# Layer 0's attention jobs: one whole job per projection unit in place of half a job

## The reference, cut to what matters

```python
proj = x @ w_in + b_in
q, k, v, h, gb, gc = jnp.split(proj, [o1, o2, o3, o4, o5], axis=-1)
...
part = banded_window_attn(q, k, v, 1, A_WINDOW, slopes)     # prompt: keys t-128..t, ALiBi
part = gathered_window_attn(q, k_all, v_all, n_hist, 1, A_WINDOW, slopes)   # samples, with a cache
y_a = combine_branches([part], sink=sink)     # softmax with a learned sink in the denominator
c = gc * h
conv = sum(c_all[:, i:i + T] * conv_w[i] for i in range(CONV_WIDTH))
y_b = gb * conv
mix = jnp.concatenate([y_a, y_b], axis=-1) @ w_out + b_out
```

## Time and profile before

| what | value |
|---|---|
| time, median of 3 runs | 2876.88 us (2871.78 to 2877.8) |
| span of the profiled execution | 2878.8 us; no other time of that execution is given |
| TensorE busy | 2724.0 us, 95% of the span |
| VectorE, ScalarE, GpSimd busy | 1022.6, 601.8, 520.3 us |
| mean granted TensorE clock | 0.973 |
| units 24 to 53 of layer 0 | from 119.81 us on |
| first store after them | 354.40 us |

### The profile page before, as it was taken

One profiled execution on the slowest core, in us unless ns is written; L12 is line 12 of the kernel. 1 busy time (PEld: TensorE's weight loads), 2 busy tenths in 40 slices (PEclk: granted clock), 3 DMA queues, 4 the chain that ended last, 5 costly groups with the idle time before them and its releaser, 6 DMA issues.

```text
span 2878.8 us, 40841 instructions
## 1 busy us (share of the span) xinstructions
PE 2724.0 (95%) x16564; PEld 2544.3 (88%) x16564; DVE 1022.6 (36%) x2244; ACT 601.8 (21%) x1297; POOL 520.3 (18%) x319
## 2 busy tenths in 40 slices
PE   7999778999999999989998999989899999999997
PEld 7989678899999999988995666669799999999996
DVE  3344325322222222264245455542722222222225
ACT  1022201411221112212002232330322111221121
POOL 2111012312121212133111000001322121212120
PEclk9999789999999999999998999999999999999998
DMA  5100031212232223212107243421113222322221
GB/s 166 58 30 30 18 80 47 84 64 92 78 116 68 90 75 116 73 66 92 37 30 225 96 147 96 140 86 58 54 64 117 68 92 73 116 73 89 78 95 63
DMA packets 79066, 240.19 MB, mean 83 GB/s; under 512 B 25568, under 2 KB 43616, under 8 KB 71648
## 3 DMA queue, kind: packets, MB, share of 16 engines
q1 hardware_dynamic: 61376, 167.65, 17.4%
q10 hardware_dynamic: 17584, 71.05, 8.3%
HBM read 224.78 MB, written 81.71 MB: 106 GB/s over the span
## 4 chain that ended last, share of the span: by engine, by line
PE 82%; DVE 8%; issue 4%; ACT 3%; DMA 2%; POOL 1%; SPq 0%; POOLq 0%; DVEq 0%; ACTq 0%
PE PS L1151 65%; PE PS L1531 2%; PE PS L1498 2%; PE PS L1467 2%; PE PS L1439 2%; PE PS L1482 1%; PE PS L1452 1%; DVE ZN L762 1%; PE PS L1180 1%; POOL WS L418 1%; DVE X L741 1%; ACT SMA L555 1%; PE PS L1238 1%; PE PS L1281 1%; DVE SMA L834 1%
## 5 line engine op out<-in xcount | busy, mean ns | idle before, releaser
L1151 PE MATMUL PS<-XS,WS 128*128 128x384 f32 (+1 forms) x8208 | 1395.8, 330 | 68.8 <-DVE XS L720 25.3
L1151 PEld LDWEIGHTS PS<-XS,WS 128*128 128x128 f32 x8208 | 1370.3, 190 | 76.9 <-issue 73.6
L1151 PE MATMUL PS<-HID,WS 128*128 128x384 f32 (+1 forms) x4608 | 765.1, 326 | 4.0 <-DVE X L941 4.0
L1151 PEld LDWEIGHTS PS<-HID,WS 128*128 128x128 f32 x4608 | 758.3, 188 | 6.1 <-DVE X L941 5.7
L418 POOL TENSOR_TENSOR WS<-WR,WS 128x1024 fp32r<-128x1024 f32 x178 | 431.0, 2421 | 1812.2 <-DVE WS L732 1060.2
L941 DVE TENSOR_TENSOR X<-X,PS 128x384 f32<-128x384 f32 (+1 forms) x384 | 203.2, 532 | 461.1 <-PE PS L1151 461.1
L926 DVE TENSOR_TENSOR HID<-ST,HID 128x384 fp32r<-128x384 f32 (+1 forms) x192 | 104.3, 543 | 632.7 <-ACT HID L604 632.7
L598 ACT ACTIVATE RT<-PS 128x384 f32<-128x384 f32 (+1 forms) x192 | 90.9, 474 | 1113.4 <-PE PS L1151 1113.4
L674 ACT ACTIVATE PTD<-PS 128x512 f32<-128x512 f32 (+2 forms) x96 | 46.9, 489 | 253.0 <-PE PS L1452 253.0
L602 ACT ACTIVATE ST<-RT 128x384 f32<-128x384 f32 (+1 forms) x192 | 97.5, 508 | 7.8
L604 ACT ACTIVATE HID<-ST 128x384 fp32r<-128x384 f32 (+1 forms) x192 | 97.5, 508 | 6.1
(11 more groups left out here) (170 smaller groups left out, 1625.4 us busy)
## 6 DMA issues: line engine op xcount, KB each, us to landing
WR<-in_w SPq DMA_DIRECT2D x178, 512.0 KB, 3.3
out_d_ks<-in_cache_d_k ACTq DMA_DIRECT2D x96, 340.0 KB
out_d_vs<-in_cache_d_v ACTq DMA_DIRECT2D x96, 340.0 KB
KCD<-in_cache_d_k SPq DMA_DIRECT2D x16, 1024.0 KB, 4.9
VCD<-in_cache_d_v SPq DMA_DIRECT2D x16, 1024.0 KB, 6.7
X<-in_x SPq DMA_DIRECT2D x4, 1536.0 KB, 9.9
TH<-in_th SPq DMA_DIRECT2D x8, 512.0 KB, 5.1
KCD<-in_cache_d_k SPq DMA_DIRECT2D x32, 128.0 KB, 4.1
```

Of the source, the lines that this page charges most:

```text
L1151: last = pe.matmul(out[:, 0:gw], WS[:, slot, a, (off + k) * P:(off + k + 1) * P], src[:, b, k, c0:c0 + gw], start=(n == 0), stop=(n == 3 * ...
```

## The change

TensorE now takes, after unit 24 + v, the odd slot 2v - 1 and the even slot 2v together: transposes of job v-1 (and transposed outputs where due), values of job v-1, and scores of job v. So job v's scores stand behind unit 24 + v for v from 0 to 16, the sample job's values behind unit 41, its transposed outputs behind unit 42. Units 43 to 53 have no attention work, and none stands behind unit 53. VectorE does the same: after every unit's evacuation from unit 24 on, `a_output` of the job before and `a_scores` of the job, and a last `a_output` after unit 41. ScalarE's, GpSimd's and SP's programs are not altered.

```diff
@@ VectorE
-                        if s >= 2:
-                            v = u - 24
-                            if v % 2 == 0:
-                                if v:
-                                    a_output(v // 2 - 1)
-                                a_scores(v // 2)
+                        if 0 <= u - 24 < N_JOBS_A:
+                            if u > 24:
+                                a_output(u - 25)
+                            a_scores(u - 24)
+                        if u - 24 == N_JOBS_A:
+                            a_output(N_JOBS_A - 1)
             for g in range(3):
                 for j in range(2):
                     u = 48 + 2 * g + j
                     ein_evac(16 + j, g, u)
                     if g == 2:
                         w_high(16 + j + NSLOT)
-                    v = u - 24
-                    if v % 2 == 0:
-                        a_output(v // 2 - 1)
-                        a_scores(v // 2)
-            for n in range(15, N_JOBS_A):
-                a_output(n - 1)
-                a_scores(n)
-            a_output(N_JOBS_A - 1)
             split_low(1, Y)
@@ TensorE
             for s in range(2, 4):
                 for g in range(3):
                     for j in range(4):
-                        unit(12 * s + 4 * g + j, 4 * s + j, g)
-                        a_slot(12 * (s - 2) + 4 * g + j)
+                        v = 12 * (s - 2) + 4 * g + j
+                        unit(24 + v, 4 * s + j, g)
+                        if 0 < v <= N_JOBS_A:
+                            a_slot(2 * v - 1)
+                        if v < N_JOBS_A:
+                            a_slot(2 * v)
+                        elif v == N_JOBS_A:
+                            a_values(N_JOBS_A - 1)
+                        elif v == N_JOBS_A + 1:
+                            pe.wait_ge(oa_evac, N_JOBS_A)
+                            pe.wait_ge(ota_evac, 8)
+                            for quad in range(2):
+                                last = pe.transpose(PS[:, 5, quad * P:quad * P + P], OTA[:, quad, :], IDN[:, :])
+                            last.then_inc(ota_mm, 1)
             for g in range(3):
                 for j in range(2):
                     unit(48 + 2 * g + j, 16 + j, g)
-                    a_slot(24 + 2 * g + j)
-            for n in range(15, N_JOBS_A):
-                a_slot(2 * n)
-                a_slot(2 * n + 1)
-            a_values(N_JOBS_A - 1)
-            pe.wait_ge(oa_evac, N_JOBS_A)
-            pe.wait_ge(ota_evac, 8)
-            for quad in range(2):
-                last = pe.transpose(PS[:, 5, quad * P:quad * P + P], OTA[:, quad, :], IDN[:, :])
-            last.then_inc(ota_mm, 1)
```

## The result

The kernel with whole jobs took 2902.32 us (median; 2895.53 to 2908.01), the kernel before beside it 2875.84: a ratio of 1.0088, with a 95% interval of 1.0067 to 1.0109. It is slower, by more than the range of the prediction allowed. A second measurement gave 2898.53 against 2878.22 (1.0074, 1.0060 to 1.0088). The profiled execution took 2895.53, its span is 2893.7, 14.9 more than before. (In every run shown here the time of an execution is 1.7 to 1.9 us over its span.)

The account below looks back on a forecast made before the run. TensorE mostly bounds the kernel, and SP's first store sets the end; some 36 of the tail's 42 us are spent again among the units, the rest at SP. Stores leave 0.3 earlier: 2876.9 - 0.3, or 2877 us; range 2871 to 2888.

Parts of the forecast that it names:

- The loop: TensorE's repeat per job among the units: 6.40 scores to transposes, 2.21 to values, 1.93 to next scores, 10.54 us.
- job 2's scores: Start of the fourteen loops on TensorE, put at 139.5 us: 146.55 - 8.3 + 1.3.
- the forecast without a fall: Granted clock stays full among the units; 2877 us, the likeliest case, chance 0.35.
- two falls or more: Rival: granted clock drops to 1.2 GHz among the units at least twice; two give 2885, four 2893; chance 0.25.
- the tail's idle 1.66 and second wait at 314 to 318: Argument against clock drops: behind the last unit, before the change, values after these waits still ran at full pace, 2.00 us.
- The rival's price: Cost of one clock drop among the units, through slower unit, values and scores: 1.1 to 5.5 us, taken as 4.
- the four slots with 320 columns: Slots among the units called worst for clock drops, having 0.69 us idle besides the copy wait.
- The sample's values: Sample job's 64 matmul records on TensorE: 6.0 us, between 5.65 and 7.0; by themselves should not lower the clock.
- SP's queue: Before the first store, tile 23 waits for GpSimd's split of tile 21: 9.2 us after unit 52 hands over at 344.9.
- The cast of tile 21: Weight cast near the units' end, claimed hidden under GpSimd's work on tile 20; otherwise costing up to 0.7 us.
- VectorE's split of Y: Split for the out projection, claimed to start a few us before the stores and hide under the reload.
- the predicted 354.1: Time in us at which SP's first store leaves, 344.9 + 9.2, against 354.40 before.

Follow-up runs that it names:

- with the stores first: Changed kernel with SP's loads of weight tiles 22 and 23 moved behind the issue of the stores: 2894.24 us, 1.0051 of the kernel before.
- the two of one kernel: Two profiled executions of the changed kernel altered to half a job per unit in the first 23 units, whole jobs in the next six: medians 2880.26 and 2873.32 us.
- the kernel with spare products: Changed kernel plus six unused 256-column matmuls behind each job's transposes, during TensorE's wait for ScalarE's copy: 2885.22 us, 1.002 of the kernel before.

## Why the prediction was wrong, point by point

- **The loop** was right: 10.54 predicted and measured, with 6.40, 2.21 and 1.93 in it, and the waits of 1.11 and 0.68. From job 2's scores (140.09, predicted 139.5) to the sample's (298.52) it is 158.43: fourteen loops of 10.53 are 147.4, and the four falls the other 11.0.
- **The failed step** is in the rivals and the chances: that the forecast without a fall has 0.35, and two falls or more 0.25. The argument against falls was that the tail's idle 1.66 and second wait at 314 to 318 were still followed by values at full pace. That was one passage, and it says nothing of sixteen on end, which the change makes. (The slow values behind it in the earlier trace rows, 3.67, do not settle it either: TensorE was idle for 4.40 before the transposes at 324.62, and in that idle time, between 321 and 322, the clock fell.) What the runs show in its place: four or five falls ahead of the sample's values in each of the three profiled executions that have whole slots only and nothing in the waits (the changed kernel twice, and with the stores first), each costing 1.3 to 2.9, and one more about the sample's values. Whether a given slot has a fall varies from execution to execution, as the two of one kernel show. The rule of the Trainium skill that stood beside this rival ("TensorE: Matmul & The Clock Gate", "A second HAM failure mode: psum-queue depth-cycling"), a clock that swings where TensorE idles briefly again and again, agrees with what these runs show: 0.7 to 1.1 us of idle in a slot of 10.5, and a clock that goes to 0.50 and back.
- **The rival's price**, 4 us a fall, was too high in the loop: 1.6 with a half-wide job, 2.2 and 2.9 else. Its mechanism, slower scores and a slower unit, was right; the values stayed at 2.00. That the four slots with 320 columns would be the worst was wrong: in the first execution one of the four has a fall, and three of the ten others.
- **The sample's values** were predicted at 6.0, at most 7.0, and measured at 9.36. At full pace 64 records of 0.114 are 7.3, so the row of 110 ns was the right end to take, not half of the slow time; the fall inside adds 2.1, and 2.0 to the unit behind. That these values by themselves should not lower the clock was wrong: in the kernel with spare products no wait stood ahead of them, and it fell. The unbroken work of the earlier trace rows had 128 columns to a load, these have 64; broken into quarters they kept the clock. That the number of columns decides was not tried alone.
- **SP's queue** was right as a mechanism: GpSimd's split of tile 21 is the last wait, and moving the two loads gains some 5 to 6 with whole jobs and nothing in the kernel before. Its size was off: 11.35 from unit 52's hand-over (360.88 to 372.23) for 9.2. The cast of tile 21, said to be hidden under the split of tile 20, started 0.30 into it and took 2.60 in place of 0.69; GpSimd waited 0.63 for it, inside the 0.7 that the prediction allowed. The split of tile 21 took 3.80 in place of 2.35 beside VectorE's split of Y, which the prediction had put at nothing.

The sum of it: the store came 18.1 after the predicted 354.1. Falls are 16.6 of that (1.6, 2.2, three times 2.9, and 4.1 about the sample's values); 2.15 are the splits and 1.3 the sample's full pace; off go 1.0 for an earlier start of unit 24 (118.81, before 119.81) and 0.7 for the sample's softmax (7.87 from scores to values for 8.6). These terms come to 0.2 more than the 18.1. The reload's way to TensorE is 1.2 longer, the rest of the kernel 4.1 shorter: 15.2 over the forecast, 14.9 over the span before. The medians lie further apart, 26.5. The profiled execution of after is 6.8 under its median, its fellows having a mean clock of 0.968 to 0.970 against its 0.972; that of before, with 1.8 added to its span, took 2880.6, 4.8 over the 2875.84.

**What stays open:** what makes the clock fall in one slot and not in the next; whether the idle time or the few columns around it weigh more (the spare products take away idle time and add columns, the scores ahead of the values take away idle time and shorten the slot); and why the stretch behind the reload was 4.1 quicker.

The gain that the change could have had is real: the jobs behind unit 53 are gone, and with the wait filled by the next scores the kernel is 0.6% faster than before, with the queue and the sample's values mended as well 0.9%. The change alone moved the waits of the tail into sixteen slots, which was nearly even by the chain, as predicted, and the clock then took some 17 us.

## What to carry to other kernels

When a change packs dependent steps closer, look at what stands in each wait that it lays bare: waits of 0.7 to 1.1 us in slots of 10.5 cost no more by the chain than was reckoned, and up to 2.9 more by the clock in the slots that had a fall. Order a slot so that the next step's independent work stands in the wait, before accepting the wait as small. And where the times of one kernel spread by more than 10 us, compare two of its profiles before reading places into one.

## What the runs showed that was not expected

- The clock falls at places that change from execution to execution of one program: four falls or none in the same six slots, 2886.2 and 2870.9 us of span.
- Spare products in the wait made the kernel faster: 2885.22 against 2898.53 and 2902.32, though nothing reads them.
- VectorE and GpSimd get in each other's way: a cast of a weight tile on VectorE that starts 0.30 after a split on GpSimd takes 2.60, 0.69 else; a split beside VectorE's subtraction of two operands takes 3.80, 2.35 to 2.41 else. The Trainium skill ("SBUF — State Buffer", "Who interferes with whom") says that the two engines share a pair of ports, and that with a VectorE instruction that uses the pair, as a cast can, whichever instruction comes first keeps the other out to its end. The cast's time agrees with it: it ends 0.55 after the split, about the 0.69 that it takes alone.
